# Sums of squares over heads: one float32 matmul, or two of the rounded format with the low half made by GpSimd

## The reference

```python
def _rms(x, g):
    xf = x.astype(jnp.float32)
    y = xf * lax.rsqrt(jnp.mean(xf * xf, axis=-1, keepdims=True) + EPS)
    return (y * g.astype(jnp.float32)).astype(x.dtype)
...
    qa = _rms(_heads(a_q, A_HEADS), a_q_g)
    ka = _rms(_heads(a_k, A_HEADS), a_k_g)
...
    yc = jax.nn.silu(c_g.astype(f32)) * _rms(_merge(oc), g_c.reshape(C_HEADS, HEAD_DIM)).reshape(bsz, t, C_DIM)
```

## Time and profile before

| | |
|---|---|
| median of 3 runs | 1088.75 us (1088.63 to 1089.39) |
| the profiled execution | 1089.28 us, its span 1087.5 us |
| TensorE matmul busy | 1074.7 us, 99% of the span |
| TensorE weight load busy | 864.5 us (79%) |
| VectorE busy | 712.2 us (65%) |
| ScalarE busy | 421.8 us (39%) |
| GpSimd busy | 0.2 us, 4 instructions |
| granted TensorE clock | 0.999 of full, mean of the span |
| the ten norms | from 125 to 198 us of the span |

### The profile page before, as it was taken

How to read it: one execution, slowest core, us unless ns; L and a number is a source line. 1 busy time by engine, 2 the same in 40 slices (tenths; PEclk the granted TensorE clock), 3 DMA queues, 4 the chain that set the end, 5 groups by cost and what they waited for, 6 DMA issues and landing times.

```text
span 1087.5 us, 13609 instructions
## 1 busy us (share of the span) xinstructions
PE 1074.7 (99%) x5401; PEld 864.5 (79%) x5403; DVE 712.2 (65%) x1148; ACT 421.8 (39%) x663; POOL 0.2 (0%) x4
## 2 busy tenths in 40 slices
PE   9999999999999999999999999999999999999998
PEld 6777877977878888888888887887776777888886
DVE  6898877868668887854588745654568446464441
ACT  6612656343442223222222234744357443323232
POOL 0000000000000000000000000000000000000000
PEclk9999999999999999999999999999999999999999
DMA  8432122121213323234322234333121222033312
GB/s 256 122 117 79 40 77 77 63 97 39 79 50 115 117 78 106 58 88 125 127 78 87 62 94 146 89 105 117 44 78 35 82 78 78 1 116 116 100 36 78
DMA packets 100239, 95.94 MB, mean 88 GB/s; under 512 B 5952, under 2 KB 91088, under 8 KB 100176
## 3 DMA queue, kind: packets, MB, share of 16 engines
q1 hardware_dynamic: 100000, 95.05, 27.9%
q10 hardware_dynamic: 176, 0.02, 0.0%
HBM read 92.95 MB, written 2.10 MB: 87 GB/s over the span
## 4 chain that ended last, share of the span: by engine, by line
PE 93%; DVE 4%; ACT 1%; issue 1%; DMA 1%; DVEq 0%; ACTq 0%
PE ring L1030 22%; PE ring L1032 22%; PE ring L1031 22%; PE bank L1030 3%; PE bank L1032 3%; PE bank L1031 3%; PE bank L1485 1%; PE bank L1280 1%; PE bank L1252 1%; DVE w_lo L1917 1%; PE bank L1185 1%; PE bank L1265 1%; PE bank L1117 1%; PE bank L1509 1%; PE bank L1458 1%
## 5 line engine op out<-in xcount | busy, mean ns | idle before, releaser
L1030 PE MATMUL ring<-act_hi,w_hi 128*128 128x512 f32 (+1 forms) x816 | 323.4, 396 | 0.9 <-DVE xT L2296 0.5
L1032 PE MATMUL ring<-act_hi,w_lo 128*128 128x512 f32 (+1 forms) x816 | 316.7, 388 | 0.0
L1031 PE MATMUL ring<-act_lo,w_hi 128*128 128x512 f32 (+1 forms) x816 | 316.4, 388 | 0.0
L1573 ACT ACTIVATE w_hi<-w_raw 128x2048 fp32r<-128x2048 f32 (+4 forms) x97 | 160.8, 1659 | 250.1 <-PE ring L1032 206.1
L1917 DVE TENSOR_TENSOR w_lo<-w_raw,w_hi 128x2048 fp32r<-128x2048 f32 (+5 forms) x102 | 191.4, 1879 | 4.0 <-ACT w_hi L1573 3.8
L1030 PEld LDWEIGHTS ring<-act_hi,w_hi 128*128 128x128 f32 x816 | 153.3, 188 | 37.5 <-issue 3.9
L1031 PEld LDWEIGHTS ring<-act_lo,w_hi 128*128 128x128 f32 x816 | 153.4, 188 | 31.7 <-issue 1.9
L1032 PEld LDWEIGHTS ring<-act_hi,w_lo 128*128 128x128 f32 x816 | 153.2, 188 | 31.7
L1030 PE MATMUL ring<-hidH,w_hi 128*128 128x512 f32 x176 | 68.5, 389 | 0.0
L1031 PE MATMUL ring<-hidL,w_hi 128*128 128x512 f32 x176 | 68.5, 389 | 0.0
L1032 PE MATMUL ring<-hidH,w_lo 128*128 128x512 f32 x176 | 68.5, 389 | 0.0
(11 more groups left out here) (358 smaller groups left out, 1615.4 us busy)
## 6 DMA issues: line engine op xcount, KB each, us to landing
w_raw<-in_w_in SPq DMA_DIRECT2D x30, 1024.0 KB, 5.3
w_raw<-in_w_up SPq DMA_DIRECT2D x22, 1024.0 KB, 5.1
w_raw<-in_w_out SPq DMA_DIRECT2D x8, 1024.0 KB, 5.1
w_raw<-in_w_down SPq DMA_DIRECT2D x8, 768.0 KB, 4.7
w_raw<-in_w_down SPq DMA_DIRECT2D x8, 640.0 KB, 4.3
w_raw<-in_w_in SPq DMA_DIRECT2D x7, 512.0 KB, 5.7
xin<-in_xt SPq DMA_DIRECT2D x8, 256.0 KB, 4.3
xT<-in_xt SPq DMA_DIRECT2D x2, 1024.0 KB, 6.5
```

Source lines behind the costliest of these rows:

```text
L1030: pe.matmul(out, ah, bh, start=(first and n == 0), stop=False)
L1031: pe.matmul(out, ah, bl, start=False, stop=False)
L1032: mm = pe.matmul(out, al, bh, start=False, stop=(last and n == len(pairs) - 1))
L1573: return act.activation(out, src, func, **more)
```

## The change

`scr` still gets the square in float32, but ScalarE first writes the same square rounded to F32R into a new buffer `sqH`; it reads its source twice. GpSimd gets a program of its own: for each n it waits for `nrm_sq` (and, from n = 2, for the matmul that read the buffer before), subtracts, `sqL = scr - sqH`, and increments a new semaphore `nrm_lo`. TensorE multiplies `sqH` by the block matrix, waits for `nrm_lo`, and adds the product with `sqL` in the same bank. The matrix is copied once to F32R (`blkR`), by ScalarE ahead of the first squares. The new buffers lie in memory that is free at that time. To make room for the semaphore, `lb_d` and `nbcf_ready` become one, which is waited for at 1 and 2; VectorE's two increments come in that order as before.

```diff
+        sqH = [sb(f"sqH{i}", [P, T], F32R, M + 22 + 2 * i) for i in range(2)]
+        sqL = [sb(f"sqL{i}", [P, T], F32R, M + (20, 26)[i]) for i in range(2)]
+        blkR = sb("blkR", [P, P], F32R, M + 10)
...
-                    pe.matmul(nrm_bank(n)[:], cc("blk"), scr[n % 2][:], start=True, stop=True).then_inc(nrm_mm, 1)
+                    pe.matmul(nrm_bank(n)[:], blkR[:], sqH[n % 2][:], start=True, stop=False)
+                    pe.wait_ge(nrm_lo, n + 1)
+                    pe.matmul(nrm_bank(n)[:], blkR[:], sqL[n % 2][:], start=False, stop=True).then_inc(nrm_mm, 1)
...
                     if kind == "hg_sq":
                         act.wait_ge(hg_o_mm, i + 1)
-                        for hh in range(2):
-                            r = slice(64 * hh, 64 * hh + 64)
-                            ins = A(scr[n % 2][r, :], bank[2 * i + hh][r, :], ACT.Square)
+                        if i == 0:
+                            A(blkR[:], cc("blk"), ACT.Identity)
+                        for to in (sqH[n % 2], scr[n % 2]):
+                            for hh in range(2):
+                                r = slice(64 * hh, 64 * hh + 64)
+                                ins = A(to[r, :], bank[2 * i + hh][r, :], ACT.Square)
                         ins.then_inc(nrm_sq, 1)
                     else:
                         src = (qT if i < 4 else kT)[:, i % 4, :]
                         of = ("a_q" if i < 4 else "a_k", i % 4)
                         act.wait_ge(z_in, z_at[of])
+                        A(sqH[n % 2][:], src, ACT.Square)
                         A(scr[n % 2][:], src, ACT.Square).then_inc(nrm_sq, 1)
...
+        @block.gpsimd
+        def _(pool):
+            for n in range(10):
+                pool.wait_ge(nrm_sq, n + 1)
+                if n >= 2:
+                    pool.wait_ge(nrm_mm, n - 1)
+                pool.tensor_tensor(sqL[n % 2][:], scr[n % 2][:], sqH[n % 2][:].bitcast(F32), ALU.subtract).then_inc(nrm_lo, 1)
```

More of the change, by code:

```diff
@@ L128, in two_blocks @@
             sem(n) for n in ("x_sq", "x_sum", "x_ss", "x_rs", "x_hi", "x_lo", "x_col", "z_in"))
-        lb_d, lb_e, nbcf_ready, mask_ready = (sem(n) for n in ("lb_d", "lb_e", "nbcf_ready", "mask_ready"))
+        lb_nbcf, lb_e, mask_ready = (sem(n) for n in ("lb_nbcf", "lb_e", "mask_ready"))
         gate_ln, gate_m, gate_rows, gate_cols, negC_ready, negB_in = (
@@ L139, in two_blocks @@
             sem(n) for n in ("hg_kd", "hg_cross_mm", "hg_sc", "hg_u_mm", "hg_u_s", "hg_scan", "hg_rep_mm", "hg_dm", "hg_in_mm", "hg_o_mm", "hg_n", "hg_done"))
-        nrm_sq, nrm_mm, nrm_rs, nrm_done, qk_done = (sem(n) for n in ("nrm_sq", "nrm_mm", "nrm_rs", "nrm_done", "qk_done"))
+        nrm_sq, nrm_lo, nrm_mm, nrm_rs, nrm_done, qk_done = (sem(n) for n in ("nrm_sq", "nrm_lo", "nrm_mm", "nrm_rs", "nrm_done", "qk_done"))
         conv_b, qkB_ready, ml_m_mm, ml_w, ml_e, ml_s_mm, ml_p, ml_o_mm, ml_o_s = (
@@ L1608, in _ @@
                     A(rsx[:], rsx[:], ACT.Exp, scale=-0.5).then_inc(x_rs, 1)
-                    act.wait_ge(lb_d, 1)
+                    act.wait_ge(lb_nbcf, 1)
                     A(lbe, lbd, ACT.Exp).then_inc(lb_e, 1)
@@ L1612, in _ @@
                     p = s[2]
-                    act.wait_ge(nbcf_ready, 1)
+                    act.wait_ge(lb_nbcf, 2)
                     act.wait_ge(bank_free(s[1:]), drains(s[1:]))
@@ L1974, in _ @@
                     dve.wait_ge(par_in, 16)
-                    TT(lbd, pc("lb", 0, 2), pc("lb", 0, 2), ALU.subtract).then_inc(lb_d, 1)
-                    TS(nbcf, pc("b_cf", 0, 2), -1.0, None, ALU.mult).then_inc(nbcf_ready, 1)
+                    TT(lbd, pc("lb", 0, 2), pc("lb", 0, 2), ALU.subtract).then_inc(lb_nbcf, 1)
+                    TS(nbcf, pc("b_cf", 0, 2), -1.0, None, ALU.mult).then_inc(lb_nbcf, 1)
                 elif kind == "params":
```

## The result

The change makes the kernel slower. Median 1092.95 us (1091.72 to 1096.28, 6 runs) against 1089.1 us (1088.63 to 1089.76, 6 runs); ratio 1.0043, interval 1.0033 to 1.0052. The forecast was 1089.0, "within 0.2%", in a range up to 1092.6: too good, and the measured median lies 0.35 us outside. Run again beside the first experiments, the change gave 1091.85 (1091.53 to 1093.46, 6 runs), ratio 1.0028, interval 1.0016 to 1.0039.

A forecast was written before the change was run, and what follows sets the result against it. TensorE was taken to bound the kernel (1074.7 of 1087.5 us). 4.05 us saved, 4.27 lost in waits at n = 2, 6 and 9: 0.2 slower, 1089.5 for the profiled execution, 1089.0 against the median; range 1087.0 to 1092.6.

The forecast's parts named there:

- "no wait" at n = 0 and 1: First two norms: the first subtraction ends at 122.9, TensorE comes only at 125.29 and doesn't wait; lead 0.81.
- The clock: TensorE's clock falling in a wait at n = 2, 6 or 9 would prove the forecast wrong; given no size.
- The 0.405 us saved per norm: TensorE, each norm: float32 matmul 0.86 us against 0.455 for two F32R matmuls; ten times, 4.05 us.
- 1.22: GpSimd's subtraction in us, taken between 0.69 (VectorE, same size) and 2.28 (VectorE, four times the width).
- 2.86: Us from start of first square to end of second matmul's turn: second square, rounding, subtraction, handoffs, weight load, turn.
- 145.14: Start of the square of n = 2, earlier by 0.405 through a chain where VectorE had waited 2.59 us for TensorE.
- rival 2: GpSimd and VectorE block each other at n = 5 and 7, costing 0.5 and 0.3; 1089.8 us; chance 0.26.
- Step two: n = 6: Square stays at 179.85, second matmul's turn ends at 182.71 against 182.21 before; lead falls from 1.33 to -0.50.
- the lead: Time by which TensorE is ahead of before at a place; 4.05 at the end with no waits, forecast -0.2.
- Step three: n = 9: Square directly follows the norm of n = 8; turn ends at 197.62, next matmul before at 197.41; lead -0.2.
- a subtraction of 2.28 us: Slow case for GpSimd at every norm: lead -3.8 at n = 9, 1092.6 us; slower by over 0.2%: chance 0.22.
- A and B: Theories of the follow-up runs: TensorE waits for the subtraction; GpSimd and VectorE exclude each other and VectorE's delay reaches TensorE.

The follow-up runs named there:

- the first experiments: Follow-up runs of variants of the change, beside which the change itself was run once more, unaltered, for its spread: 1091.85 us, ratio 1.0028.
- run 2: The change without GpSimd's subtraction, the second matmul reading `sqH` again without waiting, both squares kept, low half left out: 1086.2 us, ratio 0.9974.
- run 3: The change with GpSimd subtracting `sqH` from itself, TensorE not waiting and its second matmul reading `sqH`, low half left out: 1087.75 us.
- run 8: The change with the low half subtracted by VectorE, right behind the squares in its queue, instead of by GpSimd: 1101.76 us.

## Why the prediction was wrong

**In short.** The step that failed is "no wait" at n = 0 and 1, taken to mean that nothing is lost there, and with it a sum whose only path was square, subtraction, matmul. GpSimd's subtractions lengthened VectorE's rows, and VectorE's delay reached TensorE at n = 2 and n = 9, about 1 us each. The clock, another 1.2 us of the median, had no term in the sum.

**Right.** The 0.405 us saved per norm (run 2, with the 1.1 us at n = 6). That GpSimd's lateness wins it back. The places: n = 2, 6 and 9, and no wait at n = 3, 4, 5, 7, 8. That the program behind n = 9 moves by n = 9: 2.6 us later there, 2.4 at the end.

**Near, and partly luck.** The subtraction took 1.27 us against 1.22, a value chosen between bounds a factor of 3 apart; and it did so in six of ten places, while four took 2.06 to 2.15. The distance from the start of the first square to the next work at n = 2 is 2.87 (146.20 to 149.07) against 2.86, but the terms differ: the subtraction and its two handoffs are 0.11 longer, and the weight load and the turn together 0.09 shorter (0.33 from 148.74 to 149.07, for 0.42). The waits before L1190 are 0.84 to 0.86 each and 2.6 in all, not "1 to 2" and "some 4"; 1.8 us more stand before L1188, for ScalarE, which the forecast didn't name.

**Wrong, step one: "no wait" at n = 0 and 1 and what followed at n = 2.** The prediction looked only at TensorE, which indeed waits for nothing there. But the first two subtractions lengthened VectorE's scan and copy by 0.98 and 1.13 us, in a stretch where it is full. The projection tile behind them was taken out late, TensorE waited 0.54 us for its bank, and the chain to the square of n = 2 was no longer ahead of before:

```profile
138.12 0.19 DVE L2105 COPY small<-bank 128x32 f32<-128x32 f32 x1 [0.90 <-PE bank L1109]
...
146.20 0.61 ACT L1578 ACTIVATE sqH<-qT 128x512 fp32r<-128x512 f32 x1
```

The prediction had 145.14 for the square; VectorE's slack of 2.59 us was down to 0.90. That the subtractions are the cause is shown by run 2: with the same squares and no GpSimd the square starts where it was forecast,

```profile
145.03 0.62 ACT L1577 ACTIVATE sqH<-qT 128x512 fp32r<-128x512 f32 x1
```

and with the subtractions that nobody waits for (run 3) at 145.86. This is 1.07 us of the miss, and rival 2's mechanism at a place where the prediction hadn't looked for it: it had priced it at n = 5 and 7 only, and gave it 0.8 us in all. Run 3 gives the mechanism 1.55 us alone.

**Step two: n = 6.** From n = 5 to n = 6 the lead fell by 2.1 us; the sum had 1.8. That the lead ended at -1.85 and not at -0.50 is mostly n = 2 once more: the anchor, VectorE's copy after n = 3, stood at 165.59, where the sum had it 0.52 before 165.02. The other 0.24 lie in VectorE's second half of a `w_lo`: ready when ScalarE's rounding behind two squares was over, as forecast, and then held up by the subtraction of n = 5, which lasted until 173.97, as rival 2 said:

```profile
173.58 1.47 DVE L1935 TENSOR_TENSOR w_lo<-w_raw,w_hi 128x1024 fp32r<-128x1024 f32 x1 [0.75 <-ACT w_hi L1578]
```

A part of what is lost at n = 6 is there without GpSimd: the 1.1 us of run 2, for the two second squares. The sum had both of them, as the 0.52 of the delayed rounding and the 0.52 in the 2.86, so they are no part of the miss.

**Step three: n = 9.** The sum had the logarithm of n = 8 start when its sum is ready. It stood behind the stage `decay_in` on ScalarE, which waits for VectorE's decay rows:

```profile
195.82 0.69 ACT L1578 ACTIVATE scr<-bank,con 128x512 f32<-128x512 f32 x1 [4.04 <-DVE negB L2099]
```

The matmul's sum was ready at 194.91. Here the exclusion struck again: L2088, the first of those decay rows, took 1.44 for 0.42. Without these 1.02 us the rows would have been over at 194.62, before that sum (an estimate from these rows). The lead fell by 1.5 from n = 8 to n = 9 where the sum had 0.5: 1.0 us of the miss.

**Step four: the clock.** The prediction names it among what would make it wrong and gives it no price. It accounts for what lies above 1092.6: in half the runs the clock fell and took 1 to 4.5 us. With the profile's waits alone the time is 1091.7, inside the range, but that is luck: the upper end stood for a subtraction of 2.28 us, which is not what made it so long.

**The 3.95 us from 1089.0 to 1092.95.** The sum missed by 2.2 us (1089.5 forecast for the profiled execution, 1091.72 measured), nearly all of it VectorE's exclusion in two places. The clock is 1.2 (1091.72 to 1092.95). The last 0.5 was taken off for the median of 1088.75; the kernel before, run beside the change, had 1089.1.

**Open.** Which wait the clock falls in isn't shown for the change itself: its profiled executions are among the undisturbed ones. Nor are A and B separable to the tenth: a delay of VectorE also makes the wait of TensorE longer. Not tried: `nrm_sq` behind the first square with a second semaphore for `scr`.

## What to carry to other kernels

An idle GpSimd isn't free help: with its inputs in SBUF it takes time from VectorE's rows that read SBUF, and they from it, one full instruction at a time. Before giving it work, look at what VectorE does in that window, and who waits for VectorE's queue behind it. A saving on the busiest engine lasts only to the next place where that engine meets a chain anchored elsewhere (here ScalarE's queue, which stands behind VectorE's); count the lead from anchor to anchor. Here waits of about 1 us on TensorE went with a lower clock in some runs, so time more than one run and read the clock of each. And look at what an increment stands behind: here a matmul waited for a square that it doesn't read.

## What was not expected of the hardware

- A GpSimd subtraction of 128x512 takes 1.27 us with two different inputs and 1.04 with one tensor as both; a fill takes 0.53.
- The first GpSimd subtraction took 1.34 us: nothing like the 6 us that the Trainium skill, GPSIMD Engine Reference (2.1 Instruction dispatch), has for freshly loaded code. This trace shows no such call.
- The granted clock fell in 6 of 12 runs of the change, whose waits are 0.5 to 1.3 us, and in none of 11 with the three waits for GpSimd filled.
- In one trace (run 8) it stayed at 1.00 through a wait of 3.47 us and fell in one of 2.64 us.
